# One decoder layer with a 32-expert mixture on one core: second norm by columns, three lent buffers, the last pair's chunks alternated

## The reference, cut to what matters

```python
x = layer_norm(ALPHA * x + hybrid_mixer(x), ln1_g, ln1_b)            # x is (256, 1024)
x = layer_norm(ALPHA * x + cross_attention(x, mem), ln2_g, ln2_b)
x = layer_norm(ALPHA * x + moe_ffn(x), ln3_g, ln3_b)
# layer_norm: (x - mean) * rsqrt(var + eps) * g + b, g and b by column
# moe_ffn: the top 4 of 32 experts per token, softmax over their logits as gates;
#   h = xb @ w_gate_up[e] + b_gate_up[e]      (1024 x 2048 per expert)
#   y = ((u + 1) * g * sigmoid(1.702 g)) @ w_down[e] + b_down[e]     (1024 x 1024)
```

## Time and profile before

| | us |
|---|---|
| three executions | 1204.78, 1204.81, 1205.69 |
| the profiled execution, first to last instruction (span) | 1202.1 |
| what the median has beyond that span | 2.7 |
| PE busy | 1146.8 (95%) |
| DVE, ACT, POOL busy | 219.4, 133.3, 49.7 |
| weight queue (q1): 440.49 MB | 88.3% of 16 engines' span |

### The profile page before, as it was taken

The page is one execution under the profiler, slowest core; times in us unless marked ns, Lnnn a source line. Parts: engine busy times, 40 slices in busy tenths (PEclk is TensorE's granted clock), DMA queues, the critical chain, the costliest instruction groups (busy, mean ns, idle before and its releaser), DMA issues.

```text
span 1202.1 us, 12962 instructions
## 1 busy us (share of the span) xinstructions
PE 1146.8 (95%) x5354; PEld 522.3 (43%) x5354; DVE 219.4 (18%) x559; ACT 133.3 (11%) x281; POOL 49.7 (4%) x56
## 2 busy tenths in 40 slices
PE   9999999999999999999999999898989899999986
PEld 7686747754434343433434343333333333333322
DVE  1232122224211111121111111111111111111113
ACT  2133111222100000010000000000000000000001
POOL 0232002010000000000000000000000000000001
PEclk9999999999999999999999999999999999999998
DMA  9953334398999999999999999999999999999995
GB/s 350 323 204 141 133 112 157 122 373 326 429 429 427 427 414 429 428 429 430 427 429 427 427 428 429 429 430 427 428 428 430 429 429 427 429 430 429 427 429 215
DMA packets 55698, 446.63 MB, mean 372 GB/s; under 512 B 10304, under 2 KB 11472, under 8 KB 30192
## 3 DMA queue, kind: packets, MB, share of 16 engines
q1 hardware_dynamic: 53200, 440.49, 88.3%
q10 hardware_dynamic: 2464, 5.66, 1.3%
HBM read 445.06 MB, written 1.07 MB: 371 GB/s over the span
## 4 chain that ended last, share of the span: by engine, by line
PE 62%; DMA 35%; DVE 2%; issue 1%; SPq 0%; ACT 0%
DMA ring<-in_w_gate_up 32%; PE bank L1693 21%; PE bank L1333 9%; PE bank L1742 9%; PE bank L1320 8%; DMA ring<-in_w_down 3%; PE bank L1577 3%; PE bank L1638 2%; PE bank L1653 1%; PE bank L1367 1%; PE bank L1718 1%; PE bank L1792 1%; PE bank L1731 1%; PE bank L1519 1%; PE bank L1497 1%
## 5 line engine op out<-in xcount | busy, mean ns | idle before, releaser
L1693 PE MATMUL bank<-ring,PT 128*64 128x512 f32 x1792 | 396.5, 594 | 29.9 <-DMA ring<-in_w_gate_up 29.9
L1693 PEld LDWEIGHTS bank<-ring,PT 128*64 128x64 f32 x1792 | 125.9, 137 | 295.3 <-issue 235.4
L1182 DVE TENSOR_SCALAR reg_k<-bank 128x512 f32<-128x512 f32 x32 | 22.1, 691 | 449.9 <-PE bank L1693 444.1
L1320 PE MATMUL bank<-reg_bc,ring 128*128 128x256 f32 x448 | 99.6, 381 | 0.0
L805 ACT ACTIVATE reg_v<-reg_k 128x512 f32<-128x512 f32 x30 | 18.9, 630 | 689.3 <-DVE reg_k L1182 689.3
L1742 PE MATMUL bank<-reg_q,NCt 128*64 128x512 f32 x400 | 92.0, 602 | 0.0
L1320 PEld LDWEIGHTS bank<-reg_bc,ring 128*128 128x128 f32 x448 | 84.4, 190 | 14.1 <-issue 3.2
L1742 PE MATMUL bank<-reg_bc,NCt 128*64 128x512 f32 x400 | 90.1, 592 | 0.0
L1577 PEld LDWEIGHTS bank<-L,reg_a 128*128 128x128 f32 x512 | 62.9, 196 | 24.8 <-issue 23.5
L1577 PE MATMUL bank<-L,reg_a 128*128 128x128 f32 x512 | 69.3, 288 | 1.0 <-DVE L L1096 0.7
L1213 DVE COPY reg_v<-bank 128x512 f32<-128x512 f32 x28 | 19.4, 692 | 269.0 <-PE bank L1742 269.0
(11 more groups left out here) (232 smaller groups left out, 709.0 us busy)
## 6 DMA issues: line engine op xcount, KB each, us to landing
ring<-in_w_gate_up SPq DMA_DIRECT2D x114, 2048.0 KB, 23.3
reg_bc<-in_w_down SPq DMA_DIRECT2D x26, 2048.0 KB, 20.7
reg_q<-in_w_down SPq DMA_DIRECT2D x25, 2048.0 KB, 19.2
ring<-in_w_down SPq DMA_DIRECT2D x8, 2048.0 KB, 18.9
ring<-in_w_in SPq DMA_DIRECT2D x5, 2048.0 KB, 17.1
reg_kv<-in_w_gate_up SPq DMA_DIRECT2D x5, 2048.0 KB, 18.0
ring<-in_w_down SPq DMA_DIRECT2D x9, 1024.0 KB, 7.3
reg_q<-in_w_gate_up SPq DMA_DIRECT2D x4, 2048.0 KB, 14.2
```

Of the source, the lines that this page charges most:

```text
L1182: nc.vector.tensor_scalar(gbuf, banks[0][:, :], LIMIT, None, ALU.min).then_inc(g_ready, 1)
L1320: last = mm(B(name)[:, a * T:(a + 1) * T], w[:, k, c:c + P], src[:, k, :], start=(k == 0), stop=(k == KD - 1))
L1693: last = mm(ps[half * CAP:(half + 1) * CAP, :], xgT[:, k, i * CAP:(i + 1) * CAP], w[:, j, col:col + HALF], start=(opens and k == 0), stop= ...
```

## The change

It removes the rows of gain and bias 2 and the operations with them. x2 is replaced by `x2hat`, normalised without gain and bias, in place in `reg_v`; ACT makes all four halves. Gain and bias are loaded by columns (`lncol` 4 and 5) and applied when the gathered columns are evacuated, in four ACT operations per half instead of one. In pair 6 `base` makes alpha times gain and bias as rows, by all-ones products with diagonal tiles that POOL made, VectorE multiplies x2hat by them, and TensorE adds the results. `x_nat` and `reg_a` are lent to rows k = 0 and 1 of expert 0, `reg_k` to row 2, so `OPENING` loses chunk (0, 0) and has 35 entries; the first gate-up goes through k as 4, 5, 6, 7, 3, 2, 0, 1. The halves of the gather change places in the prefix. Norm 3's rows are loaded behind all weights. The last pair's down chunks go (30, 4), (31, 4), (30, 5), (31, 5), both in loads and in products, and the scatter of expert 30's output stands whole inside the last of them. `y3` moves to `reg_v`, `ysb`, `sig` and `repT` to `reg_a`.

```diff
-OPENING = ([(i, c) for i in range(2) for c in range(GUC)] + [(i, c) for i in range(2) for c in range(GUC, CH)]
+OPENING = ([(i, c) for i in range(2) for c in range(GUC) if (i, c) != (0, 0)]
+           + [(i, c) for i in range(2) for c in range(GUC, CH)]
...
-PIECES = [(4, 0, 2), (4, 2, 4), (5, 0, 2), (5, 2, 3), (5, 3, 4)]
+PIECES = [(0, 5, 0, 2), (0, 5, 2, 4), (1, 5, 0, 2), (1, 5, 2, 3), (1, 5, 3, 4)]
...
-        x2 = mem_nat
-        y3 = mem_nat
+        y3 = reg_v
+        diag = x_nat[:, :, :].rearrange("p s (k f) -> p s k f", k=KD)
...
-        ysb = flat_v[:, 512:1536].rearrange("p (i n) -> p i n", i=2)
+        ysb = flat_a[:, 512:1536].rearrange("p (i n) -> p i n", i=2)
...
-        sig = reg_v[:, 0, 0:512]
+        sig = flat_a[:, 0:512]
         x1 = reg_v
+        x2hat = reg_v
+        scaled_x2 = (gbuf, sig)
...
-        lent = reg_k[:, :].rearrange("p (j n) -> p j n", j=1)
+        lent = [x_nat[:, :, :].rearrange("p (j a) d -> p j (a d)", j=1), reg_a[:, :].rearrange("p (j n) -> p j n", j=1),
+                reg_k[:, :].rearrange("p (j n) -> p j n", j=1)]
...
+                elif g == "wo0":
+                    for i, v in enumerate((ln2_g, ln2_b)):
+                        sp.dma_start(lncol[:, 4 + i, :].rearrange("p (c j) -> p c j", j=GUJ),
+                                     v[0].rearrange("(c p j) -> p c j", p=P, j=GUJ)).then_inc(lncol2_in, 16)
...
+            def load_lent(k, of, arrived):
+                e, c = of
+                sp.dma_start(lent[k], chunk_source(e, c)[:, k % GUJ:k % GUJ + 1, :]).then_inc(arrived, 16)
...
-                    load_half(NSLOT, 0, ahead_in)
+                    load_half(NSLOT, 0, ahead_in[0])
+                    wait_evacuated(sp, ("wo1", 1))
+                    load_lent(0, (0, 0), lent_in[0])
+                    sp.wait_ge(ln_out, TT)
+                    load_lent(1, (0, 0), lent_in[1])
                     continue
                 if n == NSLOT - 1:
-                    sp.dma_start(lent, chunk_source(0, 0)[:, 0:1, :]).then_inc(lent_in, 16)
+                    load_lent(2, (0, 1), lent_in[2])
                 load_chunk(*OPENING[n], n)
...
-            sp.dma_start(lng[2], ln3_g.to_broadcast([P, D])).then_inc(ln_in[2], 16)
...
-            sp.dma_start(lnb[2], ln3_b.to_broadcast([P, D])).then_inc(ln_in[2], 16)
             sp.wait_ge(opened, 1)
-            load_half(NSLOT, 1, slot_in[0])
+            load_half(NSLOT + 1, 0, ahead_in[1])
             sp.wait_ge(opened, 2)
-            load_half(NSLOT + 1, 0, ahead2_in)
+            load_half(NSLOT + 1, 1, slot_in[1])
             sp.wait_ge(opened, 3)
-            load_half(NSLOT + 1, 1, slot_in[1])
+            load_half(NSLOT + 2, 0, ahead_in[2])
             sp.wait_ge(opened, 4)
...
             load_half(NSLOT + 2, 1, slot_in[2])
             sp.wait_ge(opened, 5)
...
+            load_half(NSLOT, 1, slot_in[0])
+            for n in range(NSLOT + 3, len(OPENING)):
                 wait_opening(n - NSLOT)
                 load_chunk(*OPENING[n], n)
             for c in range(CH):
-                wait_opening(OPEN * 2 * CH - NSLOT + c)
+                wait_opening(3 * NSLOT + c)
...
-            wait_used(0, NE - 1)
-            load_chunk(NE - 2, 5, FINAL[0, 5])
...
+            wait_used(1, NE - 1)
+            load_chunk(NE - 1, 4, FINAL[1, 4])
+            for piece, (i, c, j0, j1) in zip(piece_in, PIECES):
                 if j0 == 0:
...
+                    wait_used(2 * i, NE - 1)
+                sp.dma_start(slot_tile(FINAL[i, c], c)[:, j0:j1, :],
+                             chunk_source(NE - 2 + i, c)[:, j0:j1, :]).then_inc(piece, 16)
+            sp.dma_start(lng[2], ln3_g.to_broadcast([P, D])).then_inc(ln_in[2], 16)
+            sp.dma_start(lnb[2], ln3_b.to_broadcast([P, D])).then_inc(ln_in[2], 16)
...
+            pool.wait_ge(gu_done, 1)
+            for i in range(2):
+                last = nc.gpsimd.tensor_tensor(
+                    diag[:, i, :, :], K[:, C_AID:C_AID + P].rearrange("p (k f) -> p k f", k=1).to_broadcast([P, KD, P]),
+                    lncol[:, 2 + i, :].rearrange("p (k f) -> p k f", f=1).to_broadcast([P, KD, P]), ALU.mult)
+            last.then_inc(diag_ready, 1)
...
-                                     bias=nmr[:, tt:tt + 1]).then_inc(xn_ready, 1)
+                wait_filled(act, ("rT", tt, half))
+                nc.scalar.activation(x2hat[:, tt, cols], x1[:, tt, cols], ACT.Identity, scale=rstd[:, 1, tt, 1:2],
+                                     bias=nmr[:, tt:tt + 1]).then_inc(x2hat_ready, 1)
...
+            copy(("rT", 0, 0), rT[:, 0:4, :], four(("rT", 0, 0)))
             for half in range(2):
                 normalise(0, half)
-            copy(("rT", 0, 0), rT[:, 0:4, :], four(("rT", 0, 0)))
...
             std(1, 1)
             nc.scalar.activation(warm[:, 2:3], K[:, C_EPS:C_EPS + 1], ACT.Exp)
+            for half in range(2):
+                normalise(1, half)
...
             def evac_xgT(half, m):
                 act.wait_ge((xgTa_done, xgTb_done)[half], m)
...
+                for j in range(4):
+                    k = 4 * half + j
+                    last = nc.scalar.activation(xgT[:, k, :], (xy_ps, tr_ps)[half][:, j * P:(j + 1) * P], ACT.Identity,
+                                                scale=lncol[:, 4, k:k + 1], bias=lncol[:, 5, k:k + 1])
+                last.then_inc((xgTa_sb, xgTb_sb)[half], 1)
+            act.wait_ge(lncol2_in, 32)
+            evac_xgT(1, 1)
             evac_xgT(0, 1)
-            evac_xgT(1, 1)
...
-            gain2(0)
             rpart_copy(1)
             scaled(1)
...
-            scale_and_bias2(0)
             ranks(1)
             places(S, 0, False, (1,)).then_inc(s_ready, 1)
-            gain2(1)
-            scale_and_bias2(1)
...
+            def scaled_residual():
+                dve.wait_ge(h_ready, 2 * BASE_PAIR + 1)
+                for half in range(2):
+                    cols = slice(half * HALF, (half + 1) * HALF)
+                    dve.wait_ge(gain_done, half + 1)
+                    if half > 0:
+                        dve.wait_ge(scaled_used, half)
+                    for tt in range(TT):
+                        last = nc.vector.tensor_tensor(scaled_x2[tt], xy_ps[:, :], x2hat[:, tt, cols], ALU.mult)
+                    last.then_inc(scaled_ready, 1)
...
-            dve.wait_ge(chunks_used, 1)
+            dve.wait_ge(chunks_used, GUC - 1)
...
+                        scaled_residual()
...
-            pe.wait_ge(x2_pool, 2)
-            gather(0, (0,))
+            pe.wait_ge(x2hat_ready, 2)
+            gather(1, (0,))
             router_part(1, 1)
             router(1)
-            gather(1, (0,))
+            gather(0, (0,))
             def base(p):
+                pe.wait_ge(diag_ready, 1)
+                pe.wait_ge(y_sb, p * 2)
+                for half in range(2):
+                    rows = slice(4 * half, 4 * half + 4)
+                    if half > 0:
+                        pe.wait_ge(scaled_ready, half)
+                    mm(xy_ps[:, :], one, diag[:, 0, rows, :].rearrange("p k f -> p (k f)"),
+                       start=True, stop=True).then_inc(gain_done, 1)
+                    for tt in range(TT):
+                        mm(acc[tt][half][:, :], one, diag[:, 1, rows, :].rearrange("p k f -> p (k f)"),
+                           start=False, stop=False, skip_group_check=True)
+                    pe.wait_ge(scaled_ready, half + 1)
+                    for tt in range(TT):
+                        last = mm(acc[tt][half][:, :], ident, scaled_x2[tt], start=False, stop=False, skip_group_check=True)
+                    last.then_inc(scaled_used, 1)
                 pe.wait_ge(rep_ready, 1)
-                pe.wait_ge(y_sb, p * 2)
                 for j in range(2):
                     for tt in range(TT):
                         last = nc.tensor.transpose(xy_ps[0:NQ, j * T + tt * P:j * T + (tt + 1) * P], rep[:, j, tt, :], ident)
                 last.then_inc(tab_done, 1)
-                for tt in range(TT):
-                    for half in range(2):
-                        mm(acc[tt][half][:, :], K[:, C_AID:C_AID + P], x2[:, tt, half * HALF:(half + 1) * HALF],
-                           start=False, stop=False, skip_group_check=True)
                 pe.wait_ge(cand_ready, 1)
...
             def first_gate_up():
-                pe.wait_ge(xgTa_sb, 1)
...
+                pe.wait_ge(xgTb_sb, 1)
+                order = (4, 5, 6, 7, 3, 2, 0, 1)
+                for k in order:
+                    if k == 3:
+                        pe.wait_ge(xgTa_sb, 1)
...
-                    if k == 0:
...
+                    if k < 3:
+                        pe.wait_ge(lent_in[k], 16)
+                        w = lent[k][:, 0, :]
                     else:
...
+                        w = chunk(0, 0, c, "open")[:, j, :]
...
+                    if k >= 3:
                         last.then_inc(opened, 1)
...
+                    elif k == 2:
```

(75 more changed lines are left out.)

74 lines of the change are left out of this document (14 added, 60 removed).

## The result

| | before | after |
|---|---|---|
| median of four runs, us | 1204.80 (1204.48 to 1205.69) | 1211.40 (1210.51 to 1212.45) |
| profiled execution, span | 1202.1 | 1208.9 |
| last weights landed | 1186.86 | 1193.31 |
| first statistics of norm 3 | 1190.69 | 1198.48 |

The ratio is 1.0056, with a 95% interval of 1.0044 to 1.0068: slower by 0.56%, 0.7 us above the 1210.7 predicted.

The account below looks back on a forecast made before the run. DMA at 428 GB/s was taken to bound the kernel from 302 us, with PE's releases deciding where spare is small. DMA 4.9 us late plus tail 1.0 gave +5.9 on 1204.8: 1210.7 us, range 1205.5 to 1213.5.

Parts of the forecast that it names:

- Start: Start of the experts: four ACT operations instead of one delay the first gate-up product from 284.72 to 284.95, +0.25 us.
- Stall per pair: Each pair's second half: ACT's longer evacuation of gather(0) delays h and the down product, +0.7 us of PE (0 to 0.9).
- Place 1: Issue at 448.00, chunk 0 of expert 7: spare 0.35 us, PE 1.65 late, so DMA 1.3 late.
- Up to the base: PE's lateness reaching the base pair, after stalls and the absorbing waits for weights: 1.7 us.
- The base: Base pair: ten products instead of four, +5.15, and uncovered table transposes, +1.9; 7.05 us in all (5.2 to 8.5).
- Place 2: Issue at 641.12 in the base pair: release 8.75 us late, spare 3.9, so DMA 4.9 late from there on.
- The tail: Last pair's new order leaves VectorE's copy of the last down output uncovered; statistics +1.0 us (0.5 to 1.5).
- The lead: 2 MiB more loaded into lent buffers before the experts, 4.9 us of DMA; claimed worth nothing beyond 448 us.
- The prediction's own rule: Spare of a load TensorE releases: previous landing minus (issue + 2.7 us fixed); lateness beyond it makes DMA late.
- table load: Rival: Identity following Sigmoid on ACT loads a table each pair, 1.28 us per switch, stall about 2.0; 1218 us, chance 0.03.
- The lead survives: Rival: PE's release at 448 us doesn't bind, DMA stays 2 MiB ahead to the end; 1200.9 us, chance 0.07.
- everything but the tail is hidden: Rival: ACT's longer evacuation stalls nothing and the base finds cover or spare; only +1.0 remains, 1205.8 us, chance 0.10.

Follow-up runs that it names:

- Experiment 3: Also dve_columns: the changed kernel with gather(0)'s columns scaled and evacuated by VectorE instead of ACT; 1211.12 us, 1.0049 of the kernel before.
- Experiment 1: Also no_bias_rows: the changed kernel without the base's four products that add the bias rows; 1211.91 us, 1.0056 of the kernel before.
- experiment 4: Also tail_old: the changed kernel with the last pair's down chunks loaded and used in the old order; 1210.25 us, 1.0045 of the kernel before.
- before_nine_long: The kernel before with nine buffers used through expert 11 and the base in pair 5; 1204.25 us, 0.9999 of the kernel before.
- experiment 9: Also split_base: the changed kernel with its base divided, tables in pair 6 and residual in pair 9; 1207.92 us, 1.0027 of the kernel before.
- lent_late: The changed kernel with lent rows 0 and 1 of expert 0 loaded behind all buffers; 1212.30 us, 1.0060 of the kernel before.
- nine_long_all: The changed kernel with nine buffers through expert 11, base in pair 5, VectorE evacuating gather(0) and the old last pair; 1208.23 us, 1.0031 of the kernel before.
- split_nine_all: The changed kernel with divided base (pairs 8, 12), nine buffers through expert 11, VectorE evacuating gather(0), old last pair; 1205.20 us, 0.9998 of the kernel before.
- nine_long: The changed kernel with nine buffers used through expert 11 instead of 5 and the base in pair 5; 1212.85 us, 1.0069 of the kernel before.

## Why the prediction was right, point by point

- **Start.** Predicted +0.25; the first gate-up product starts at 284.97 instead of 284.72, exactly that, but partly by luck. S was ready 0.23 earlier than assumed and ACT began at 283.21 instead of 283.38; the product, in return, started 0.26 behind the end of ACT's fourth operation (284.71), where the prediction had 0.07. Why it took longer isn't shown.
- **Stall per pair.** Predicted 0.7, measured 0.68 in the pair read, and a wait of this kind stands in 14 pairs. Experiment 3 removed it at its source.
- **Place 1.** Predicted issue about 449.7 and DMA 1.3 late; measured 449.58 and 1.26.
- **Up to the base.** Predicted 1.7 late; it starts at 625.57 against 623.93: 1.64.
- **The base.** Predicted 7.05 us, measured 11.15 - 3.9 = 7.25. The size was right and one reason incomplete. With the bias products in place they do cover VectorE's multiplications, as predicted. But I priced the rest by TensorE's count, so I expected the time to fall if products were removed. Experiment 1 showed that the two paths are nearly equally long (11.08 and 11.15), so that the count gave the right sum by luck.
- **Place 2.** Predicted release 8.75 late and DMA 4.9 late; measured 9.0 and 5.2.
- **The tail.** Predicted 1.0 (0.5 to 1.5), measured 1.34. The removed cover is the wait of 0.80 ahead of L1656; with the old order (experiment 4) it is gone.
- **The lead.** That it would be worth nothing was right, the place was mostly wrong. I wrote that it "is worth nothing beyond 448 us". The ledger has 3.8 of 4.8 us gone by 377; only the last 1.1 went at place 1. DMA moves only 294 GB/s from 284 to 300 us and 240 from 300 to 304: behind 293.80 nothing is issued until 302.39, while TensorE first reads the lent rows (L1731, from 293.57 on) and frees no buffer. The prediction's own rule finds this place. It says "Two places have little" spare, but the trace of the kernel before has 2.7 at the issue of 302.15 and 2.5 at that of 333.19, both less than place 2's 3.9 and than the lead of 4.9. A lead can't be longer than the spare of the next load that TensorE releases. The backlog that it called "some 20 us" is 17 (24.7 less 7.6); that changes nothing.
- **What the sum missed.** From place 2 to the end DMA lost another 1.2 us, and the last stores ended 1.0 us sooner behind the same chain of the third norm. So the sum of 5.9 stands against 6.4 + 1.3 - 1.0 = 6.8 in the profiled span and 6.6 in the medians. The 1.2 are one transfer of 6.4 us right behind place 2 (5.4 in the kernel before) and small ones. The 1.0 belongs to the change: the last store of SP's queue lands 3.7 us after its issue in before and before_nine_long and 2.7 in all ten of the changed kernels, which store from `reg_v` instead of `reg_a`; the cause isn't shown. That 1.2 and 1.0 nearly cancel is luck.
- **Rivals.** No table load appears between 300 and 1170 us, with Identity behind Sigmoid in every pair: L806's four operations take 1.51, as L733's did. The Trainium skill (ScalarE: Activation LUTs, Table sets: the hidden batching unit) says that cheap functions, identity among them, are in every table set. By that no load is due, and the trace agrees. "The lead survives" is refuted by the ledger, and "everything but the tail is hidden" by the ledger too (5.2 of 6.4 us stand ahead of the tail at place 2) and by experiment 9.

What remains open: the prediction treats 8.75 as one number, but in seven of the ten profiled kernels with the changed base the down biases ran at a lower granted clock (5.38 us instead of 3.68), so a single profile of the base is uncertain by 1.7 us. The kernel after was profiled in an execution without it; how often its other executions had it isn't known.

## What to carry to other kernels

Where a queue of transfers runs at its rate, price added work not by its length but against the spare of the release behind it: previous landing less issue less fixed part. Work over that spare costs the difference at once and for good; the same work, in two portions each under the spare, costs almost nothing (0.2 us at this place in experiment 9). Bytes loaded ahead into lent space help only up to the next load that TensorE's progress releases: whatever of the lead is over that load's spare is lost there (here 4.9 us against 2.7). And removing one tight place only pays if the next one has spare for the lateness that is carried on.

## What the runs showed of the hardware

**TensorE's clock fell behind the small products of the base.** In the kernel after, behind the waits of the base (PE's windows: stretch, busy PE, granted clock, DMA share, GB/s):
```profile
642.00:644.00 2.00, 1.49 (x10) 0.92 1.08 459
644.00:646.00 2.00, 2.00 (x6) 0.50 0.96 410
646.00:648.00 2.00, 2.00 (x8) 0.73 0.58 246
```
The granted clock is 0.50, the lower level of 1.2 GHz, after a stretch in which PE waited 1.86 and 0.72 us with small matmuls between. The products there take longer, by the timeline:
```profile
643.58 2.01 PE L1671 MATMUL bank<-L 64*128 64x512 f32 x4
```
where 1.13 stands in the other pairs. The kernel before pays the same (2.08 at 634.66) behind a wait of 0.72 alone, so it is no part of the difference; but in no_bias_rows, dve_columns, tail_old, lent_late, nine_long_all and both divided bases it fell once more, right behind the table chain, which made the down biases 1.7 us longer. In before and before_nine_long, which have no wait at that place, it didn't fall there. So an uncovered wait can have a price beyond its length. Why it fell in some executions of the same code and not in others was not found.

**Instruction packets lie in slow transfers.** Most 2 MiB transfers follow each other by 4.9 us. In split_nine_all two took 6.1. The **DMA view** of 960 to 968 us, in which one of them ran:
```profile
q1 hardware_dynamic: 237, 3.38, 99.5%
q8 instruction: 1, 0.02, 0.8%
```
(packets, MB, share): one packet of an instruction queue beside the weights. I counted this over the twelve profiled kernels, for transfers issued from 300 to 1140 us with more than 1 us of spare: all 69 that took over 5.03 us have such a packet between 2 us before their start (the previous landing) and their landing. Of the packets, 191 in all in that stretch, most came without a slow transfer. The 6.4 us behind place 2 in the kernel after, and the 6.0 behind the new place of nine_long, are among the 69. The page counts 0.43 MB on this queue in the kernels before and after, 0.49 in split_base and 0.59 in split_nine_all, which have more pairs outside of loops. The coincidence is counted; that the packets cause the delay was not tried, since no run took them away.

**The time to landing of a lone transfer varies.** At places 1 and 2 and their like, with nothing else queued, 2 MiB landed after 7.6 to 8.1 us, but after 8.6 in dve_columns. At 302 us they took 8.3 to 8.9 in all ten changed kernels; each of these ten had one of the instruction packets above between issue and landing, the others had none. With a fixed part of 2.7 us a spare is therefore good to some 0.5 us, and place 1's 0.35 was within that.
